# Attention with query weights split on GpSimd, the query bias on ScalarE, and reordered scores and last blocks

## The chip, the cores and the metric

The kernel runs on one core of a Trainium2 chip. The metric is the device time of the whole program in microseconds. A core has TensorE (matmul, PE in the profile), VectorE (DVE), ScalarE (ACT), GpSimd (POOL) and a queue for transfers on SyncE (SP); each works through its own instruction list in order, and they meet through semaphores.

## The reference, cut to what matters

The program is two transformer blocks on 512 tokens of width 1024. The second one ends with a sliding-window attention of 16 query heads over 4 key/value heads, and that attention is what the change touches:

```
q = (h @ w_q + b_q) * 64 ** -0.5               # 16 heads of 64
s = q @ k.T - slope * dist                     # a block of 128 queries against 256 keys
s = where(band and valid, s, -inf)
m = maximum(max(s), sink)
p = exp(s - m)
denom = sum(p) + exp(sink - m)
o = (p @ v) / denom
return o @ w_o + b_o
```

Before it come the keys and values (`kv`), behind it the last feed-forward network. All is in float32.

## The kernel before, in words

**Layout.** Activations are stored with features on the 128 partitions and the 512 tokens along a row, a width of 1024 being eight tiles of 128x512. A float32 matrix product is made of three matmuls of reduced-precision operands: with W = W_hi + W_lo and X = X_hi + X_lo it adds W_hi X_hi, W_hi X_lo and W_lo X_hi. A *unit* is one output tile of 128 features: eight blocks of 128 input features, 24 matmuls of 512 columns.

**Weights.** They stream through four slots. SyncE loads 512 KB into `raw` for slot s (line 1723) once the slot's last low part is made; ScalarE writes W_hi (`split_hi`, line 221, once the slot's last unit is done); the low part W_lo = raw - W_hi is `split_lo` (line 226) on VectorE. `ahead` makes the split two units before it is due. In the first block eleven such low parts are made on GpSimd instead (line 2249).

**Attention.** The 16 heads are eight pairs, pair t being the two heads (e = 0, 1) of query tile t. Per pair:

- TensorE computes the query tile, one unit (`part`, in pieces between other work). VectorE evacuates it from PSUM times the token's norm into the buffer `AW` (`evacuate`, line 1054, semaphore `evac`), and then adds the bias and scales into `QT` (line 1450, semaphore `q_t`).
- `scores_pe` (line 1283) computes scores in two halves n of two query blocks each, both heads, into banks 2 and 3. The second half needs the first to be evacuated (`s_sc`). `scored` (line 1459) evacuates on VectorE and adds the distance term. `maxima` (lines 1468, 1470) follow for e = 0, 1.
- `exps` (lines 1385, 1389) on ScalarE: exponentials and their sums for one head.
- `normalise` (lines 1478 to 1485) on VectorE divides by the sum, four instructions for one head, semaphore `s_n`.
- `transpose_pe` (line 1295) turns the probabilities, `by_keys` (line 1399) on ScalarE copies them, `values_pe` (line 1308) multiplies with the values. ScalarE writes the high part of the output tile (line 1415, `t_hi`), VectorE the low part (line 1491, `t_lo`).

The loop over t runs on each engine by hand-written order: in step t VectorE works on pair t+1's scores and on query tile t+2, TensorE on pair t+1's scores, on unit t+2, and on pair t's transposes and values. The three cuts in `attention_pe` say how many of the eight blocks of unit t+2 stand before the second half's scores, between the transposes, and before the values. Units 8 and 9 are the first two of the output projection (`U_BO`); all but their last two blocks can run inside the loop, and `residual_pe` does the rest.

Of the kernel before, what the change touches and what calls it, by code (L numbers as in the profile page):

```python
# [22 lines left out]
ACT = mybir.ActivationFunctionType  # L23
# [7 lines left out]
KT = D // P  # L31
# [55 lines left out]
def build(nc, io):  # L87
    with ExitStack() as ctx:
# [140 lines left out]
        def split_lo_half(dve, r, s, part):  # L229

            if part == 0:
                dve.wait_ge(S(f"w_hi{s}"), count(f"w_hi{s}", r + 1))
            c = slice(s * 1024 + part * 512, s * 1024 + (part + 1) * 512)
            last = nc.vector.tensor_tensor(w_lo[:, c], raw[:, c], w_hi[:, c].bitcast(F32), ALU.subtract)
            if part:
                last.then_inc(S(f"w_lo{s}"), 1)

        def ahead(eng, split, r, k):
# [819 lines left out]
        def residual_pe(pe, base, pair, wait, n=KT, late=2, begun=False, closing=False):  # L1058
            if begun:
                for s in range(2):  # L1060
                    part_blocks(pe, s, s, pair, n - late, n, n, wait).then_inc(S(f"unit_done{s}"), 1)
            else:
                two_units(pe, rnd(base, 0), pair, wait, late, n)
            for i in range(2):
                for s in range(0 if i else 2, SLOTS - (closing and i)):
                    unit(pe, rnd(base, i), s, pair, n)
# [188 lines left out]
        MX = carve(96)  # L1255
        DD = carve(T)

        def sc3(t, e):
# [54 lines left out]
        def attention_pe(pe):  # L1313
# [32 lines left out]
            scores_pe(pe, 0, 0)  # L1346
            part(1, 2, 5)
            scores_pe(pe, 0, 1)
            part(1, 5, KT)
            part(2, 0, 2)  # L1350
            for t in range(KT):
                cuts = (0, 2, 5, KT) if t else (2, 4, 6, KT)
                if t < KT - 1:
                    scores_pe(pe, t + 1, 0)
                part(t + 2, cuts[0], cuts[1])
                if t < KT - 1:
                    scores_pe(pe, t + 1, 1)
                transpose_pe(pe, t, 0)
                part(t + 2, cuts[1], cuts[2])
                transpose_pe(pe, t, 1)  # L1360
                part(t + 2, cuts[2], cuts[3])
                values_pe(pe, t)

            residual_pe(pe, U_BO, pairA, wait_o, late=2, begun=True)

        def attention_act(act):
# [25 lines left out]
            def by_keys(t, e):  # L1392

                if t > 1:
                    act.wait_ge(S("s_o"), count("s_o", t - 1))
                for n in range(2):
                    act.wait_ge(S("s_tr"), count("s_tr", 4 * t + 2 * e + n + 1))
                    lo = 0 if n else P
                    a.activation(PT[t % 2][e][:, n * T + lo:(n + 1) * T], ps[4 + n][:, lo:T], ACT.Copy)\
                        .then_inc(S("s_pt"), 1)  # L1400
            for k in range(2):
                ahead(act, split_hi, rnd(U_Q, 0), k)
            for e in range(2):
                exps(0, e)
            for t in range(KT):
# [3 lines left out]
                if t < KT - 1:  # L1409
                    exps(t + 1, 0)  # L1410
                by_keys(t, 1)
                if t < KT - 1:
                    exps(t + 1, 1)
# [4 lines left out]
        def attention_dve(dve):  # L1418
            v = nc.vector
            for k in range(2):  # L1420
                ahead(dve, split_lo, rnd(U_KV, 0), k)
# [7 lines left out]
            for e in range(2):  # L1429
                for p in range(2):  # L1430
                    v.memset(SC[p][e][:, 0:P], -FAR).then_inc(S("zeros"), 1)
                v.tensor_copy(DD[:, e * 256:(e + 1) * 256], cst[:, C_DIST:C_DIST + 256]).then_inc(S("zeros"), 1)
            dve.wait_ge(S("zeros"), count("zeros", ZEROS + 6))
            dve.wait_ge(S("kv_R"), count("kv_R", 1))
# [8 lines left out]
            def q_tile(t):  # L1443

                r, k = rnd(U_Q, t // SLOTS), t % SLOTS
                if t:
                    dve.wait_ge(S("q_t"), count("q_t", t))
                evacuate(dve, r, k, AW, 1.0, R[:])
                dve.wait_ge(S(f"evac{k}"), count(f"evac{k}", r + 1))
                v.tensor_scalar(QT[t % 2], AW, par_col("b_q", t), 0.125, ALU.add, ALU.mult).then_inc(S("q_t"), 1)  # L1450

# [41 lines left out]
            q_tile(0)  # L1493
            ahead(dve, split_lo, rnd(U_Q, 0), 0)
            scored(0, 0)
            ahead(dve, split_lo, rnd(U_Q, 0), 1)
            scored(0, 1)
            maxima(0, 0)
            q_tile(1)
            maxima(0, 1)  # L1500
            normalise(0, 0)
            normalise(0, 1)
            for t in range(KT):
                more = t < KT - 1
                if more:
                    scored(t + 1, 0)
                if t < KT - 2:
                    ahead(dve, split_lo, rnd(U_Q, (t + 2) // SLOTS), (t + 2) % SLOTS)
                if t:
                    output_lo(t - 1)  # L1510
                if more:
                    scored(t + 1, 1)
                    maxima(t + 1, 0)
# [179 lines left out]
        def second_block_pool(pool):  # L1693
# [7 lines left out]
            sum_squares(pool, "kv", KT)  # L1701
            token_rsqrt(pool, "kv")
            sum_squares(pool, "n_f1", KT)
            token_rsqrt(pool, "n_f1")
# [693 lines left out]
```

## Time and profile before

| | |
|---|---|
| median of 3 runs | 1967.9 us (1967.87 to 1968.82) |
| profiled execution | 1968.16 us, of which the span of the profile is 1966.1 |
| busy: TensorE | 1894.2 us, 96% |
| busy: VectorE | 1205.2 us, 61% |
| busy: ScalarE | 787.6 us, 40% |
| busy: GpSimd | 280.2 us, 14% |
| mean granted clock of TensorE | 0.988 of full |

The page gives busy time per engine over the whole program, which is an average over stages that differ much. The attention loop takes about 110 us of it, from 1444 to 1553 us. A timeline lists instructions in order of time, with start and duration; in square brackets stands how long the engine had been idle and which engine and line ended that. PEclk in a table of windows is the share of full clock granted to TensorE: 1.00 is 2.4 GHz, 0.50 is 1.2 GHz.

### The profile page before, as it was taken

Reading aid. Unit: us, or ns where it says so; the run is one execution under the profiler, and the core shown is the slowest. Engines: PE = TensorE matmul, PEld = TensorE weight load, DVE = VectorE, ACT = ScalarE, POOL = GpSimd, SP = SyncE. Lnnn points to the kernel's source line nnn. Section 1 sums busy time; section 2 is a strip of 40 time slices with the busy share of each in tenths; the row PEclk is TensorE's granted clock in tenths of the full one; section 3 lists DMA queues with packets and bytes.
Section 4 is the critical chain, followed back from the end, with each engine's and each line's share of the span. In section 5 each row is a group of like instructions: output and inputs, shape, how many; then the busy total and the mean of one; then the engine's idle time right before and its main releaser. Section 6 shows DMA issues by size and latency. Waiting matters only on the chain.

```text
span 1966.1 us, 29676 instructions
## 1 busy us (share of the span) xinstructions
PE 1894.2 (96%) x10634; PEld 1528.4 (78%) x10634; DVE 1205.2 (61%) x1846; ACT 787.6 (40%) x1494; POOL 280.2 (14%) x215
## 2 busy tenths in 40 slices
PE   7999899999999899999989999999999999999997
PEld 5888678888887677777768788888777788888886
DVE  5996544333333777767745756737678657567474
ACT  4233344232233554555533433424536534234242
POOL 2533222011012200000111100101100011001012
PEclk9999999999999899999999999999999999999998
DMA  5232323232323111111112232222311122322322
GB/s 185 94 106 85 109 85 97 96 103 90 106 87 97 44 55 60 60 60 60 50 44 86 97 107 86 96 97 96 125 58 44 63 77 96 110 89 92 103 91 82
DMA packets 46945, 170.47 MB, mean 87 GB/s; under 512 B 5344, under 2 KB 5504, under 8 KB 46720
## 3 DMA queue, kind: packets, MB, share of 16 engines
q1 hardware_dynamic: 45648, 165.12, 25.6%
q10 hardware_dynamic: 1200, 3.95, 0.6%
q8 instruction: 74, 1.21, 0.3%
q14 instruction: 23, 0.19, 0.0%
HBM read 166.94 MB, written 2.11 MB: 86 GB/s over the span
## 4 chain that ended last, share of the span: by engine, by line
PE 75%; DVE 6%; ACT 4%; issue 2%; POOL 1%; DVEq 0%; POOLq 0%; ACTq 0%
PE ps L255 16%; PE ps L256 16%; PE ps L257 16%; PE ps L267 7%; PE ps L269 5%; PE ps L268 5%; DVE scr L1217 1%; PE ps L622 1%; DVE scr L892 1%; ACT scr L1389 1%; ACT Y L1389 1%; PE ps L646 1%; PE ps L666 1%; PE ps L306 1%; DVE scr L1468 1%
## 5 line engine op out<-in xcount | busy, mean ns | idle before, releaser
L226 DVE TENSOR_TENSOR w_lo<-w_raw,w_hi 128x1024 fp32r<-128x1024 f32 x265 | 361.3, 1366 | 184.9 <-ACT w_hi L221 184.8
L221 ACT ACTIVATE w_hi<-w_raw 128x1024 fp32r<-128x1024 f32 x304 | 316.5, 1049 | 244.1 <-PE ps L257 169.2
L255 PE MATMUL ps<-A_hi,w_hi 128*128 128x512 f32 x950 | 369.8, 389 | 2.0 <-issue 1.9
L257 PE MATMUL ps<-A_hi,w_lo 128*128 128x512 f32 x950 | 369.6, 389 | 0.0
L256 PE MATMUL ps<-A_lo,w_hi 128*128 128x512 f32 x950 | 369.6, 389 | 0.0
L255 PE MATMUL ps<-B_hi,w_hi 128*128 128x512 f32 x724 | 282.9, 391 | 3.2 <-issue 2.4
L257 PE MATMUL ps<-B_hi,w_lo 128*128 128x512 f32 x724 | 281.8, 389 | 0.0
L256 PE MATMUL ps<-B_lo,w_hi 128*128 128x512 f32 x724 | 281.8, 389 | 0.0
L255 PEld LDWEIGHTS ps<-A_hi,w_hi 128*128 128x128 f32 x950 | 178.3, 188 | 40.0 <-issue 3.1
L257 PEld LDWEIGHTS ps<-A_hi,w_lo 128*128 128x128 f32 x950 | 178.3, 188 | 37.2
L256 PEld LDWEIGHTS ps<-A_lo,w_hi 128*128 128x128 f32 x950 | 178.3, 188 | 36.8
L267 PE MATMUL ps<-A_hi,w_hi 128*128 128x512 f32 x434 | 188.6, 435 | 18.0 <-DVE w_lo L226 12.7
L269 PE MATMUL ps<-A_hi,w_lo 128*128 128x512 f32 x434 | 171.0, 394 | 0.0
L268 PE MATMUL ps<-A_lo,w_hi 128*128 128x512 f32 x434 | 170.3, 392 | 0.0
L1054 DVE SCALAR_TENSOR_TENSOR scr<-ps,R 128x512 f32<-128x512 f32 x157 | 107.7, 688 | 95.8 <-PE ps L257 86.0
L255 PEld LDWEIGHTS ps<-B_hi,w_hi 128*128 128x128 f32 x724 | 135.9, 188 | 34.4 <-issue 6.3
L257 PEld LDWEIGHTS ps<-B_hi,w_lo 128*128 128x128 f32 x724 | 135.9, 188 | 28.4
L256 PEld LDWEIGHTS ps<-B_lo,w_hi 128*128 128x128 f32 x724 | 135.9, 188 | 27.9 <-issue 0.2
L267 PEld LDWEIGHTS ps<-A_hi,w_hi 128*128 128x128 f32 x434 | 81.9, 189 | 39.7 <-issue 20.1
L1054 DVE SCALAR_TENSOR_TENSOR X<-ps,X 128x512 f32 (+1 forms) x56 | 38.5, 687 | 99.8 <-PE ps L257 88.4
L267 PE MATMUL ps<-B_hi,w_hi 128*128 128x512 f32 x236 | 96.8, 410 | 2.9 <-POOL B_lo L1049 1.7
L269 PEld LDWEIGHTS ps<-A_hi,w_lo 128*128 128x128 f32 x434 | 81.8, 188 | 18.4
(289 smaller groups left out, 2563.7 us busy)
## 6 DMA issues: line engine op xcount, KB each, us to landing
w_raw<-d_ws SPq DMA_DIRECT2D x304, 512.0 KB, 3.5
X<-d_xT SPq DMA_DIRECT2D x4, 512.0 KB, 7.5
X<-d_xT ACTq DMA_DIRECT2D x1, 2048.0 KB, 8.1
d_out<-X SPq DMA_DIRECT2D x4, 512.0 KB, 2.6
scr<-gc_rows ACTq DMA_DIRECT2D x7, 256.0 KB, 3.1
cst<-d_cst SPq DMA_DIRECT2D x1, 800.0 KB, 12.6
par<-d_par SPq DMA_DIRECT2D x1, 344.5 KB, 3.3
scr<-d_pw SPq DMA_DIRECT2D x1, 256.0 KB, 12.4
```

The source lines that it names most:

```text
L221: nc.scalar.activation(w_hi[:, c], raw[:, c], ACT.Copy).then_inc(S(f"w_hi{s}"), 1)
L226: nc.vector.tensor_tensor(w_lo[:, c], raw[:, c], w_hi[:, c].bitcast(F32), ALU.subtract)\
L255: pe.matmul(ps[bank][:], w_hi[:, c], hi, start=k == 0, stop=False)
L256: pe.matmul(ps[bank][:], w_hi[:, c], lo, start=False, stop=False)
L257: last = pe.matmul(ps[bank][:], w_lo[:, c], hi, start=False, stop=k == n - 1)
L267: pe.matmul(ps[bank][:], w_hi[:, c], hi, start=k == 0, stop=False)
L268: pe.matmul(ps[bank][:], w_hi[:, c], lo, start=False, stop=False)
L269: last = pe.matmul(ps[bank][:], w_lo[:, c], hi, start=False, stop=k == total - 1)
L306: pe.matmul(out, w_hi[:, c], tile(pair[0], k), start=k == 0, stop=False)
L622: last = pe.matmul(ps[4 - c // 2][:, (c % 2) * 256:(c % 2 + 1) * 256], KQv[:, c, 0, :], KQ[:, c * 256:(c + 1) * 256], start=True, stop=True)
L1054: return nc.vector.scalar_tensor_tensor(out=out, in0=ps[k % 2 if bank is None else bank][:], scalar=scalar, in1=in1, op0=op0, op1=op1).the ...
L1389: a.activation(sc, sc, ACT.Exp, bias=neg[:, b:b + 1], accum_out=den[:, b:b + 1])\
```

## The change

The low parts of units 2 to 9 of the query and output weights go from VectorE to GpSimd (`split_lo_pool`); from the third on they also wait until pair m - 4 is normalised. VectorE evacuates a query tile as before, but the bias is now added on ScalarE (`query_bias`), with a bias column `QB` that VectorE scales once. In step 0 the second half of pair 1's scores is evacuated before pair 0 is normalised, and TensorE's cuts for steps 0 and 7 and for unit 1 are new. At the end block 6 of both output units stands before block 7 of either.

```diff
@@ -234,6 +234,13 @@
             last = nc.vector.tensor_tensor(w_lo[:, c], raw[:, c], w_hi[:, c].bitcast(F32), ALU.subtract)
             if part:
                 last.then_inc(S(f"w_lo{s}"), 1)
+
+        def split_lo_pool(pool, r, s):
+
+            pool.wait_ge(S(f"w_hi{s}"), count(f"w_hi{s}", r + 1))
+            c = slice(s * 1024, (s + 1) * 1024)
+            nc.gpsimd.tensor_tensor(w_lo[:, c], raw[:, c], w_hi[:, c].bitcast(F32), ALU.subtract)\
+                .then_inc(S(f"w_lo{s}"), 1)
 
         def ahead(eng, split, r, k):
 
@@ -1056,10 +1063,7 @@
 
 
         def residual_pe(pe, base, pair, wait, n=KT, late=2, begun=False, closing=False):
-            if begun:
-                for s in range(2):
-                    part_blocks(pe, s, s, pair, n - late, n, n, wait).then_inc(S(f"unit_done{s}"), 1)
-            else:
+            if not begun:
                 two_units(pe, rnd(base, 0), pair, wait, late, n)
             for i in range(2):
                 for s in range(0 if i else 2, SLOTS - (closing and i)):
@@ -1254,6 +1258,7 @@
         PT = [[carve(2 * T) for _ in range(2)], [Y[:, 2 * (2 + e) * T:2 * (3 + e) * T] for e in range(2)]]
         MX = carve(96)
         DD = carve(T)
+        QB = carve(8)
 
         def sc3(t, e):
             return SC[t % 2][e].rearrange("p (b s) -> p b s", b=NCH)
@@ -1344,24 +1349,31 @@
             part(1, 0, 2)
             pe.wait_ge(S("v_t"), count("v_t", 2))
             scores_pe(pe, 0, 0)
-            part(1, 2, 5)
+            part(1, 2, 4)
             scores_pe(pe, 0, 1)
-            part(1, 5, KT)
+            part(1, 4, KT)
             part(2, 0, 2)
             for t in range(KT):
-                cuts = (0, 2, 5, KT) if t else (2, 4, 6, KT)
+                cuts = (2, 6, 7, KT) if t == 0 else (0, 2, 5, KT) if t < KT - 1 else (0, 1, 3, KT)
                 if t < KT - 1:
                     scores_pe(pe, t + 1, 0)
-                part(t + 2, cuts[0], cuts[1])
+                part(t + 2, cuts[0], cuts[1] - 2 * (t == 0))
                 if t < KT - 1:
                     scores_pe(pe, t + 1, 1)
+                if t == 0:
+                    part(t + 2, cuts[1] - 2, cuts[1])
                 transpose_pe(pe, t, 0)
                 part(t + 2, cuts[1], cuts[2])
                 transpose_pe(pe, t, 1)
                 part(t + 2, cuts[2], cuts[3])
                 values_pe(pe, t)
 
-            residual_pe(pe, U_BO, pairA, wait_o, late=2, begun=True)
+            for k in (KT - 2, KT - 1):
+                for s in range(2):
+                    last = part_blocks(pe, s, s, pairA, k, k + 1, wait=wait_o)
+                    if k == KT - 1:
+                        last.then_inc(S(f"unit_done{s}"), 1)
+            residual_pe(pe, U_BO, pairA, wait_o, begun=True)
 
         def attention_act(act):
             a = nc.scalar
@@ -1398,10 +1410,18 @@
                     lo = 0 if n else P
                     a.activation(PT[t % 2][e][:, n * T + lo:(n + 1) * T], ps[4 + n][:, lo:T], ACT.Copy)\
                         .then_inc(S("s_pt"), 1)
+            def query_bias(t):
+
+                act.wait_ge(S(f"evac{t % SLOTS}"), count(f"evac{t % SLOTS}", rnd(U_Q, t // SLOTS) + 1))
+                if t > 1:
+                    act.wait_ge(S("s_p"), count("s_p", 2 * t - 2))
+                a.activation(QT[t % 2], AW, ACT.Identity, scale=0.125, bias=QB[:, t:t + 1]).then_inc(S("q_t"), 1)
+            query_bias(0)
             for k in range(2):
                 ahead(act, split_hi, rnd(U_Q, 0), k)
-            for e in range(2):
-                exps(0, e)
+            exps(0, 0)
+            query_bias(1)
+            exps(0, 1)
             for t in range(KT):
                 if t < KT - 2:
                     ahead(act, split_hi, rnd(U_Q, (t + 2) // SLOTS), (t + 2) % SLOTS)
@@ -1409,6 +1429,8 @@
                 if t < KT - 1:
                     exps(t + 1, 0)
                 by_keys(t, 1)
+                if t + 2 < KT:
+                    query_bias(t + 2)
                 if t < KT - 1:
                     exps(t + 1, 1)
                 act.wait_ge(S("s_o"), count("s_o", t + 1))
@@ -1417,6 +1439,9 @@
 
         def attention_dve(dve):
             v = nc.vector
+
+            def par_range(name, n):
+                return par[:, _cols[name][0]:_cols[name][0] + n]
             for k in range(2):
                 ahead(dve, split_lo, rnd(U_KV, 0), k)
             for m in range(4):
@@ -1430,7 +1455,8 @@
                 for p in range(2):
                     v.memset(SC[p][e][:, 0:P], -FAR).then_inc(S("zeros"), 1)
                 v.tensor_copy(DD[:, e * 256:(e + 1) * 256], cst[:, C_DIST:C_DIST + 256]).then_inc(S("zeros"), 1)
-            dve.wait_ge(S("zeros"), count("zeros", ZEROS + 6))
+            v.tensor_scalar(QB, par_range("b_q", 8), 0.125, None, ALU.mult).then_inc(S("zeros"), 1)
+            dve.wait_ge(S("zeros"), count("zeros", ZEROS + 7))
             dve.wait_ge(S("kv_R"), count("kv_R", 1))
             for k in range(SLOTS):
                 r = rnd(U_KV, 0)
@@ -1446,8 +1472,6 @@
                 if t:
                     dve.wait_ge(S("q_t"), count("q_t", t))
                 evacuate(dve, r, k, AW, 1.0, R[:])
-                dve.wait_ge(S(f"evac{k}"), count(f"evac{k}", r + 1))
-                v.tensor_scalar(QT[t % 2], AW, par_col("b_q", t), 0.125, ALU.add, ALU.mult).then_inc(S("q_t"), 1)
 
             def scored(t, n):
 
@@ -1491,25 +1515,24 @@
                 v.tensor_tensor(tile(pairA[1], t), ps[6 + t % 2][:], tile(pairA[0], t).bitcast(F32), ALU.subtract)\
                     .then_inc(S("t_lo"), 1)
             q_tile(0)
-            ahead(dve, split_lo, rnd(U_Q, 0), 0)
             scored(0, 0)
-            ahead(dve, split_lo, rnd(U_Q, 0), 1)
             scored(0, 1)
             maxima(0, 0)
             q_tile(1)
             maxima(0, 1)
-            normalise(0, 0)
-            normalise(0, 1)
             for t in range(KT):
                 more = t < KT - 1
                 if more:
                     scored(t + 1, 0)
-                if t < KT - 2:
-                    ahead(dve, split_lo, rnd(U_Q, (t + 2) // SLOTS), (t + 2) % SLOTS)
-                if t:
+                if t == 0:
+                    scored(1, 1)
+                    normalise(0, 0)
+                    normalise(0, 1)
+                else:
                     output_lo(t - 1)
+                    if more:
+                        scored(t + 1, 1)
                 if more:
-                    scored(t + 1, 1)
                     maxima(t + 1, 0)
                     maxima(t + 1, 1)
                     normalise(t + 1, 0)
@@ -1700,6 +1723,10 @@
             ffn_pool(pool, 0, U_FFN0, pairB)
             sum_squares(pool, "kv", KT)
             token_rsqrt(pool, "kv")
+            for m in range(2, 2 + KT):
+                if m > 3:
+                    pool.wait_ge(S("s_n"), count("s_n", 8 * (m - 4) + 8))
+                split_lo_pool(pool, rnd(U_Q, m // SLOTS), m % SLOTS)
             sum_squares(pool, "n_f1", KT)
             token_rsqrt(pool, "n_f1")
             ffn_pool(pool, 1, U_FFN1, pairA)
```

ScalarE, step 1 of the loop, behind pair 1's last transposed half; before (L1399 `by_keys`, L1385 and L1389 `exps` of pair 2's second head, L1415 the output's high part, L221 a weight's high part):

```order
L1399 ACTIVATE Y<-ps 128x384 [waits s_tr]
L1399 ACTIVATE Y<-ps 128x512 [waits s_tr]
L1385 ACTIVATE scr<-scr,small 128x4 [waits s_mx]
L1389 ACTIVATE scr<-scr 128x128
L1389 ACTIVATE scr<-scr 128x256 x3
L1415 ACTIVATE A_hi<-ps 128x512 [waits s_o]
L221 ACTIVATE w_hi<-w_raw 128x1024 [waits unit_done2,raw_in2]
```

After (the same are L1411, L1397, L1401, L1437, L221; L1418 is `query_bias`, waiting for VectorE's `evac3`):

```order
L1411 ACTIVATE Y<-ps 128x384 [waits s_tr]
L1411 ACTIVATE Y<-ps 128x512 [waits s_tr]
L1418 ACTIVATE scr<-scr 128x512 [waits s_p,evac3]
L1397 ACTIVATE scr<-scr,small 128x4 [waits s_mx]
L1401 ACTIVATE scr<-scr 128x128
L1401 ACTIVATE scr<-scr 128x256 x3
L1437 ACTIVATE A_hi<-ps 128x512 [waits s_o]
L221 ACTIVATE w_hi<-w_raw 128x1024 [waits unit_done2,raw_in2]
```

The bias of query tile 3 stands between the transposed half and the exponentials of the second head.

VectorE, from behind pair 2's first normalisation to pair 3's second half of scores; before (L1478 to L1485 `normalise`, L1054 evacuation, L1450 bias, L1459 scores, L226 the weight's low part, L1491 the output's low part):

```order
L1054 SCALAR_TENSOR_TENSOR scr<-ps,R 128x512 [waits unit_done3,q_t]
L1450 TENSOR_SCALAR scr<-scr,par 128x512 [waits evac3]
L1478 TENSOR_TENSOR scr<-scr 128x4 [waits s_e]
L1480 RECIPROCAL scr<-scr 128x4 [waits s_n]
L1484 TENSOR_SCALAR scr<-scr 128x128 [waits s_n]
L1485 TENSOR_TENSOR scr<-scr 128x768
L1459 SCALAR_TENSOR_TENSOR Y<-scr,small,ps 128x384 [waits s_tr,s_p]
L1459 SCALAR_TENSOR_TENSOR Y<-scr,small,ps 128x384
L226 TENSOR_TENSOR w_lo<-w_raw,w_hi 128x1024 [waits w_hi2]
L1491 TENSOR_TENSOR A_lo<-ps,A_hi 128x512 [waits t_hi]
L1459 SCALAR_TENSOR_TENSOR Y<-scr,small,ps 128x512 [waits s_tr,s_p]
L1459 SCALAR_TENSOR_TENSOR Y<-scr,small,ps 128x512
```

After (the same are L1502 to L1509, L1061, L1483, L1515):

```order
L1061 SCALAR_TENSOR_TENSOR scr<-ps,R 128x512 [waits unit_done3,q_t]
L1502 TENSOR_TENSOR scr<-scr 128x4 [waits s_e]
L1504 RECIPROCAL scr<-scr 128x4 [waits s_n]
L1508 TENSOR_SCALAR scr<-scr 128x128 [waits s_n]
L1509 TENSOR_TENSOR scr<-scr 128x768
L1483 SCALAR_TENSOR_TENSOR Y<-scr,small,ps 128x384 [waits s_tr,s_p]
L1483 SCALAR_TENSOR_TENSOR Y<-scr,small,ps 128x384
L1515 TENSOR_TENSOR A_lo<-ps,A_hi 128x512 [waits t_hi]
L1483 SCALAR_TENSOR_TENSOR Y<-scr,small,ps 128x512 [waits s_tr,s_p]
L1483 SCALAR_TENSOR_TENSOR Y<-scr,small,ps 128x512
```

L1450 and L226 are gone from between; the rest keeps its order.

GpSimd, behind the norm of the keys and values, where nothing stood before until the next norm:

```order
L440 TENSOR_TENSOR tok<-tok,mhalf 128x4 [waits norm_ms]
L242 TENSOR_TENSOR w_lo<-w_raw,w_hi 128x1024 [waits w_hi2]
L242 TENSOR_TENSOR w_lo<-w_raw,w_hi 128x1024 [waits w_hi3]
L242 TENSOR_TENSOR w_lo<-w_raw,w_hi 128x1024 [waits w_hi0,s_n]
L242 TENSOR_TENSOR w_lo<-w_raw,w_hi 128x1024 [waits w_hi1,s_n]
L242 TENSOR_TENSOR w_lo<-w_raw,w_hi 128x1024 [waits w_hi2,s_n]
L242 TENSOR_TENSOR w_lo<-w_raw,w_hi 128x1024 [waits w_hi3,s_n]
```

Eight such rows are new; those from the third on also wait for `s_n`.

## Rows read from the trace of the kernel before

**Rows 1.** Timeline of VectorE, one pair: start us, us, instruction [idle before <-releaser].

```profile
1484.04 1.13 DVE L1459 SCALAR_TENSOR_TENSOR Y<-scr,small,ps 128x384 f32<-128x384 f32 x2
1485.10 1.22 DVE L226 TENSOR_TENSOR w_lo<-w_raw,w_hi 128x1024 fp32r<-128x1024 f32 x1
...
1486.83 1.39 DVE L1459 SCALAR_TENSOR_TENSOR Y<-scr,small,ps 128x512 f32<-128x512 f32 x2
...
1491.85 0.16 DVE L1478 TENSOR_TENSOR scr<-scr 128x4 f32<-128x4 f32 x1 [0.84 <-ACT Y L1389]
...
1493.33 0.68 DVE L1054 SCALAR_TENSOR_TENSOR scr<-ps,R 128x512 f32<-128x512 f32 x1
1494.04 0.49 DVE L1450 TENSOR_SCALAR scr<-scr,par 128x512 f32<-128x512 f32 x1
1494.75 0.16 DVE L1478 TENSOR_TENSOR scr<-scr 128x4 f32<-128x4 f32 x1 [0.22 <-ACT Y L1389]
...
1496.23 1.13 DVE L1459 SCALAR_TENSOR_TENSOR scr<-scr,small,ps 128x384 f32<-128x384 f32 x2
```

**Rows 2.** Timeline of VectorE: first evacuations of pairs 2 and 7.

```profile
1471.86 1.13 DVE L1459 SCALAR_TENSOR_TENSOR scr<-scr,small,ps 128x384 f32<-128x384 f32 x2
...
1532.80 1.13 DVE L1459 SCALAR_TENSOR_TENSOR Y<-scr,small,ps 128x384 f32<-128x384 f32 x2
...
1535.16 1.40 DVE L1459 SCALAR_TENSOR_TENSOR Y<-scr,small,ps 128x512 f32<-128x512 f32 x2 [0.64 <-PE ps L1283]
```

**Rows 3.** Timeline of ScalarE, the same pair as rows 1.

```profile
1491.72 0.95 ACT L1399 ACTIVATE scr<-ps 128x384 f32<-128x384 f32 x2
1492.57 0.29 ACT L1385 ACTIVATE scr<-scr,small 128x4 f32<-128x4 f32 x1
```

**Rows 4.** Timeline of ScalarE: two activations of 512 columns.

```profile
1554.14 0.61 ACT L390 ACTIVATE SQ<-X 128x512 f32<-128x512 f32 x1
...
1613.48 0.82 ACT L1164 ACTIVATE scr<-scr,half 128x512 f32<-128x512 f32 x1
```

**Rows 5.** Timelines of ScalarE, of TensorE's weight loads and of VectorE, the start.

```profile
1452.95 0.30 ACT L1385 ACTIVATE scr<-scr,small 128x4 f32<-128x4 f32 x1 [5.87 <-DVE scr L1470]
...
1454.08 0.52 PEld L1283 LDWEIGHTS ps<-scr 64*128 64x128 f32 x8 [0.82 <-DVE scr L1450]
...
1463.77 1.21 DVE L1468 TENSOR_REDUCE scr<-Y 128x4 f32<-128x1024 f32 x1
```

**Rows 6.** Timelines of TensorE and VectorE, the end of the stage.

```profile
1551.49 0.47 PE L267 MATMUL ps<-A_hi,w_hi 128*128 128x512 f32 x1 [0.62 <-DVE A_lo L1491]
...
1552.74 0.74 DVE L1054 SCALAR_TENSOR_TENSOR X<-ps,par,X 128x512 f32<-128x512 f32 x1
...
1553.60 0.19 PEld L255 LDWEIGHTS ps<-A_hi,w_hi 128*128 128x128 f32 x1 [0.22 <-issue]
```

**Rows 7.** Timeline of TensorE, and windows: us, busy of PE, PEld, DVE, ACT, POOL; PEclk, DMA.

```profile
203.09 0.47 PE L1799 MATMUL ps<-B_hi,w_hi 128*128 128x512 f32 x1 [2.82 <-DVE X L2085]
...
1084.68 0.47 PE L255 MATMUL ps<-A_hi,w_hi 128*128 128x512 f32 x1 [1.94 <-issue]
...
1460.32 2.08 PE L1283 MATMUL ps<-scr 64*128 64x256 f32 x8 [3.71 <-DVE Y L1459]
...
1497.42 1.13 PE L1283 MATMUL ps<-scr 64*128 64x256 f32 x8 [0.30 <-DVE scr L1459]
...
202.00:204.00 2.00, 0.91 (x3) 0.80 (x4) 1.86 (x3) 0.00 (x0) 0.00 (x0) 0.87 0.00 0
204.00:206.00 2.00, 2.00 (x6) 1.52 (x6) 0.00 (x0) 0.00 (x0) 0.00 (x0) 0.50 0.41 113
```

**Rows 8.** Timelines of GpSimd and VectorE near 124 us, and the summary of L226.

```profile
124.69 2.40 POOL L2249 TENSOR_TENSOR w_lo<-w_raw,w_hi 128x1024 fp32r<-128x1024 f32 x1 [2.81 <-ACT w_hi L221]
...
122.92 4.69 DVE L2035 SCALAR_TENSOR_TENSOR ps<-Y,par,ps 128x512 f32<-128x512 f32 x7
...
L226 DVE TENSOR_TENSOR w_lo<-w_raw,w_hi x265: 1185/1226/2308, 10.2 to 1942.7; 128x1024 fp32r<-128x1024 f32 x133
```

## Prediction

> **What bounds the kernel now.** I read the page first: TensorE is busy nearly everywhere and the chain that ended last is mostly its, so a change pays only where TensorE waits. The windows over the attention stage (about 1444 to 1553 us) show it waiting there, so I took the timelines of the engines for one pair of head tiles and looked for the engine without holes. That is VectorE [rows 1]. One pair runs from the first score evacuation (L1459, 384 wide) at 1484.04 to the next one's at 1496.23: 12.19 us. VectorE has two holes in it, 0.84 before the first normalisation and 0.22 before the second, both for exponentials. The same step recurs with the same period: 1471.86 to 1532.80 is five pairs, 60.94 us [rows 2]. TensorE waits for VectorE in the same pair (0.30 before the scores at 1497.42 [rows 7]). So the attention stage is one chain: VectorE's evacuations and maxima, ScalarE's exponentials, VectorE's normalisations. The question for each edit is what it does to that chain.
>
> I call pair t the two heads of query tile t. For each pair VectorE normalises half 0, evacuates the query tile two pairs on, and normalises half 1.
>
> **The low parts go to GpSimd.** L226, started at 1485.10, delays what is behind it by 1.13 us (it overlaps its neighbours by 0.1) [rows 1]. It leaves VectorE in each of the five periods. But it was cover: between the first half's evacuation and the second half's, TensorE must compute the second half's scores into the same banks. In the last pair there is no L226, and there the second evacuation waits 0.64 for TensorE: 1535.16 - 1532.80 = 2.36 us from evacuation to evacuation, where a pair with L226 has 1486.83 - 1484.04 = 2.79 [rows 1, 2]. So the gain is 0.43 us per pair, not 1.13. GpSimd needs 2.40 us for such a part [rows 8]; it starts when the pair's normalisation and the high part are done and ends about 0.3 us later than VectorE's did. TensorE reads it two pairs on and the weight slot is refilled for use four pairs on, so this costs nothing on SyncE's queue. If GpSimd fell behind, TensorE's wait for w_lo would show it; it has 12 us for each.
>
> Beside GpSimd's 2.40 us VectorE does the next pair's score evacuation and output part, both with one operand from PSUM. In a stretch where GpSimd splits weights from 124.69, seven such instructions take 4.69 us, 0.67 each, and no longer than elsewhere [rows 8]. I count 0; the other end is L226 itself, which ranges from 1.185 to 2.308 us over the trace. The Trainium skill (GPSIMD Engine Reference, Key points) says GpSimd contends with VectorE instructions that have two SBUF inputs or run in a two-port mode. By it L226 suffers and evacuations don't, as the rows have it; the normalisation would suffer, and the new wait for s_n keeps it out of the way.
>
> **The bias goes to ScalarE.** This is the step that decides. Before, L1450 (0.49 us on VectorE, at 1494.04) ended before ScalarE's second exponentials did: the second normalisation waited 0.22 more for those [rows 1]. Removing it gains nothing on the chain. What comes in its place is on ScalarE, in front of the second exponentials, and waits for VectorE's evacuation (evac), which itself stands behind the first normalisation. ScalarE was ready for the second exponentials at 1492.57, only 0.72 us after the first normalisation began at 1491.85 [rows 1, 3]; the evacuation ends at 1493.33 + 0.68 = 1494.01. From the start of the first normalisation to that of the second:
> before 1494.75 - 1491.85 = 2.90 us [rows 1].
> After: normalisation 1.48 (1491.85 to 1493.33), evacuation 0.68, hand-over 0.03 (ScalarE's first exponentials start that soon behind the maxima), the bias 0.62, exponentials to normalisation 2.18 (1492.57 to 1494.75): 4.99 us. That is 2.09 longer.
> The bias is not in the trace. The nearest rows are Identity of the same width with scale and bias both from a column (0.82) and a square with neither (0.61) [rows 4]; I take 0.72, half-way. The next instruction on ScalarE starts 0.10 before such a one ends (1491.72 + 0.95 against 1492.57 [rows 3]), so 0.62 on the chain, bounds 0.51 and 0.72. The Trainium skill (ScalarE: Activation LUTs, What ACT_TABLE_LOAD costs) gives 280 ns and 0.833 ns an element for a bias from a column, an estimate of 0.71 us for this one; no row here shows it, and the sum doesn't need it. Identity already runs in the same kernel, and the order shows no further table load.
> Net per period 2.09 - 0.43 = 1.66 us, times five: +8.3 us.
>
> **The start.** Two things gain: the second half of pair 0's scores comes after two blocks instead of three (three matmuls; nine take 2.1 us from 1551.49 to 1553.60 [rows 6], so 0.7), and pair 1's scores no longer wait behind pair 0's normalisations. One loses: query_bias(1) stands behind the first exponentials. These begin at 1452.95 - 0.7 = 1452.25 [rows 5] and take 2.1 on ScalarE (2.18 to the normalisation, less the hand-over); the bias then ends 0.72 later at 1455.1, and TensorE, which started these scores at 1454.08 [rows 5], starts at 1455.15. Then 1.13 for the scores, as in the row at 1497.42 [rows 7], 2.36 from evacuation to evacuation and 1.3 for the second one, as in pair 7 [rows 2]: the first normalisation starts at 1459.9, and after two of 1.48 the maxima of pair 1 at 1462.9. Before they started at 1463.77 [rows 5]: 0.9 gained. The 3.71 us wait of TensorE before 1460.32 goes [rows 7]; shorter ones of 1 to 2 us stand in its place. Then the same serial step, 2.09, makes it +1.2 us at the evacuation that started at 1471.86.
>
> **The end.** Pair 7 has no query tile behind it: nothing changes in it. The cuts move blocks behind the last transposes, the same number in all. Running block 6 of both units before block 7 of either fills 0.68 us of TensorE's wait for the last output (0.62 at 1551.49 [rows 6]). But the next unit started at 1553.60, just behind the evacuation of unit 0 (1552.74 + 0.74 = 1553.48), and still needs it: unit 0's last block comes no earlier. I count 0, between 0 and -0.2.
>
> **The sum.** 1.2 + 8.3 + 0 = +9.5 us. The profiled run took 1968.16 us (span 1966.1 and 2.06 around it), the median is 1967.9. So span about 1975.6, profiled run 1977.7, median 1977.4, 0.5% slower. The bounds of the bias (six times 0.1) and of the start and end give 1976.1 to 1978.5 for this case.
>
> **Rivals.**
> *The clock falls.* TensorE's wait before the second half's scores grows from 0.30 (row at 1497.42) by 1.66, and by 0.20 because the query comes that much sooner after the first evacuation (0.43 for the missing L226, less 0.23 by which the bias ends later behind the normalisation, 2.91 against 1494.04 + 0.49 - 1491.85 = 2.68 [rows 1]): 2.16 us. A wait of 2.82 was followed by the lower level (0.50, which is 1.2 GHz) after 204 us, one of 1.94 before 1084.68 was followed by a first matmul at the usual 0.47, and after the one of 3.71 the eight score matmuls took 2.08 instead of 1.13 [rows 7]. So a fall is possible here, and costs 0.95 on the chain at once and some tenths for late transposes. TensorE at half rate then has no spare time in that pair, so at most every second pair: three falls, +3 to +4, 1980.4 to 1981.4. The Trainium skill (TensorE: Matmul & The Clock Gate, What's actually happening) says that an idle TensorE drops to 1.2 GHz and needs sustained work to return; the rows agree, and don't settle 2.16.
> *GpSimd slows VectorE after all.* If evacuations beside it stretch as L226 did at its worst (2.31 for 1.2), the first evacuation pair of 1.04 costs 0.9 more in five periods: +4.6, 1982. Rows 8 speak against it.
> *Not slower: ScalarE isn't held up.* If the evacuation were done by the time ScalarE is through with the transposed half (0.72 after the first normalisation starts, not 2.16), only the gains remain: five times 0.43 and 0.9, -3.1 us, 1964.8. The place is the wait for evac in front of the second exponentials, the point from which it decides is a wait of 1.44 us there. For it speaks that VectorE is the fullest engine and loses work; against it the order, where the bias stands ahead of those exponentials and the evacuation behind the normalisation. TensorE's waits bound what could be gained beyond that: they are under 1 us a pair.
>
> **Chances.** A measurement of this kernel tells no change from one of 0.2%, 3.9 us. The serial step alone 0.66, with falls of the clock 0.16, with GpSimd's contention 0.06, not slower 0.12. The first three are slower by over 0.2% but for a rest: slower 0.87, same 0.10, faster 0.03. The time is that of the first, 1977.4; the range goes down to 1975.0, where the first would end if the serial step were shorter by 0.4 us in each of the six, and up to 1982.5 for the second and third, and leaves the last out.
>
> **What would show it.** In the profile after: the second L1385-line exponentials of pairs 1 to 6 start about 2.8 us after the first normalisation, not 0.7, right behind the bias; ScalarE idles about 1.4 us before the bias, released by VectorE's evacuation; VectorE waits about 2.8 us before each second normalisation (0.22 before); the period is 13.85 us (12.19); the bias takes 0.6 to 0.8; score evacuations beside GpSimd stay at 0.6 to 0.74. Wrong if the period is 12 or less, or if the second normalisations follow the first within 3 us. A period over 15 with a clock below 1.00 in the windows is the second case.

## The result and the profile after

The changed kernel takes 1981.99 us (median of 4 runs, 1980.88 to 1983.11), the kernel before 1968.36 in the same comparison: a ratio of 1.0065 with a 95% interval of 1.0052 to 1.0078. It is slower by 13.6 us. The forecast was 1977.4 us, slower, with a range of 1975.0 to 1982.5. The profiled execution took 1980.88 us, its span is 1979.1, against 1966.1 before.

Timeline of VectorE in the changed kernel, one pair from first score evacuation to first score evacuation (start us, us, instruction, idle before and its releaser); it answers to [rows 1]:

```profile
1515.80 1.13 DVE L1483 SCALAR_TENSOR_TENSOR Y<-scr,small,ps 128x384 f32<-128x384 f32 x2
...
1518.17 1.41 DVE L1483 SCALAR_TENSOR_TENSOR Y<-scr,small,ps 128x512 f32<-128x512 f32 x2 [0.64 <-PE ps L1288]
...
1523.20 0.17 DVE L1502 TENSOR_TENSOR scr<-scr 128x4 f32<-128x4 f32 x1 [0.84 <-ACT Y L1401]
...
1524.68 0.68 DVE L1061 SCALAR_TENSOR_TENSOR scr<-ps,R 128x512 f32<-128x512 f32 x1
1528.20 0.16 DVE L1502 TENSOR_TENSOR scr<-scr 128x4 f32<-128x4 f32 x1 [2.84 <-ACT Y L1401]
...
1529.68 1.13 DVE L1483 SCALAR_TENSOR_TENSOR scr<-scr,small,ps 128x384 f32<-128x384 f32 x2
```

The pair takes 13.88 us instead of 12.19. Evacuation to evacuation is 2.37 (2.79 before), with the 0.64 of waiting for TensorE that [rows 2] showed in the last pair. From the first normalisation to the second (both L1502) it is 5.00 us (2.90 before), and the wait in front of the second went from 0.22 to 2.84 us.

Timeline of ScalarE in the changed kernel, the same pair; it answers to [rows 3]:

```profile
1523.07 0.95 ACT L1411 ACTIVATE scr<-ps 128x384 f32<-128x384 f32 x2
1525.40 0.72 ACT L1418 ACTIVATE scr<-scr 128x512 f32<-128x512 f32 x1 [1.38 <-DVE scr L1061]
1526.03 0.28 ACT L1397 ACTIVATE scr<-scr,small 128x4 f32<-128x4 f32 x1
```

ScalarE is through with the transposed half at 1524.02 and stands still for 1.38 us until VectorE's evacuation is done; the bias takes 0.72, the next instruction follows 0.63 after its start. The exponentials that VectorE waits for begin 2.83 us after the first normalisation, where it had been 0.72.

That is the forecast's mechanism with its numbers. What it did not have is in the stage's first third. VectorE and GpSimd there, then TensorE:

```profile
1461.55 1.22 DVE L1492 TENSOR_REDUCE scr<-Y 128x4 f32<-128x1024 f32 x1
1462.80 1.31 DVE L1494 TENSOR_SCALAR scr<-scr,small 128x4 f32<-128x4 f32 x1
...
1465.26 0.23 DVE L1494 TENSOR_SCALAR scr<-scr,small 128x4 f32<-128x4 f32 x1
```

```profile
1461.71 2.37 POOL L242 TENSOR_TENSOR w_lo<-w_raw,w_hi 128x1024 fp32r<-128x1024 f32 x1 [11.73 <-DVE scr L1509]
```

```profile
1466.72 1.55 PE L1313 MATMUL ps<-scr 128*64 128x128 f32 x22 [3.35 <-ACT scr L1411]
...
1488.21 1.98 PE L1288 MATMUL ps<-scr 64*128 64x256 f32 x8 [2.19 <-DVE Y L1483]
...
1503.11 1.13 PE L1288 MATMUL ps<-scr 64*128 64x256 f32 x8 [2.18 <-DVE scr L1483]
```

L1494, four columns wide, takes 1.31 us instead of 0.23. It ends at 1464.11, as GpSimd's low part of unit 4 does (1464.08). Everything behind it comes 1.08 us later, and TensorE waits 3.35 us in front of pair 0's values. Then its clock falls. Windows of the changed kernel (us, busy of PE, PEld, DVE, ACT, POOL; PEclk, DMA share, GB/s):

```profile
1456.00:1468.00 12.00, 7.24 (x57) 5.42 (x58) 9.61 (x19) 4.64 (x14) 2.37 (x1) 0.99 0.12 45
1468.00:1482.00 14.00, 13.43 (x78) 9.72 (x76) 9.15 (x18) 8.24 (x25) 2.37 (x1) 0.76 0.10 38
1482.00:1496.00 14.00, 11.27 (x70) 8.59 (x67) 8.64 (x19) 8.22 (x25) 2.34 (x1) 0.88 0.11 39
1496.00:1510.00 14.00, 11.82 (x86) 8.82 (x84) 9.38 (x19) 8.13 (x26) 2.35 (x1) 1.00 0.13 39
```

It is granted 0.76 of full in the second and 0.88 in the third, and 1.00 from then on. The second fall comes with a wait of 2.19 us, and costs: the eight matmuls take 1.98 instead of 1.13.

To add it up, the span is cut at the evacuation of query tile 0, at the first score evacuation of pair 2, at that of pair 7 and at the evacuation of output unit 0. All numbers are starts of VectorE's instructions, of the profiled executions:

| us | before | after | difference | forecast |
|---|---|---|---|---|
| up to query tile 0 | 1443.74 | 1442.16 | -1.58 | 0 |
| start, to pair 2 | 28.12 | 30.65 | +2.53 | +1.2 |
| five pairs | 60.94 | 70.75 | +9.81 | +8.3 |
| end, from pair 7 | 19.94 | 19.96 | +0.02 | 0 |
| the rest | 413.36 | 415.58 | +2.22 | 0 |
| span | 1966.1 | 1979.1 | +13.0 | +9.5 |

The five pairs took 14.21, 14.90, 13.88, 13.88 and 13.88 us.

### The profile page after: what moved, and what is told of

Same layout as the page of the kernel before. It is cut to its first block, busy times and chain, and to the rows that moved or that the text cites. A ratio compares the mean times of both kernels' runs of the same rounds, so it can differ in the third digit from the quotient of the medians.

```text
span 1979.1 us, 29689 instructions
## 1 busy us (share of the span) xinstructions
PE 1897.2 (96%) x10634; PEld 1530.6 (77%) x10634; DVE 1195.1 (60%) x1831; ACT 793.1 (40%) x1502; POOL 298.8 (15%) x223
## 4 chain that ended last, share of the span: by engine, by line
PE 75%; DVE 7%; ACT 4%; issue 2%; POOL 1%; DVEq 0%; POOLq 0%; ACTq 0%
PE ps L262 16%; PE ps L263 16%; PE ps L264 16%; PE ps L274 7%; PE ps L276 5%; PE ps L275 5%; DVE scr L1221 1%; PE ps L629 1%; DVE scr L899 1%; ACT scr L1401 1%; PE ps L653 1%; ACT Y L1401 1%; PE ps L1288 1%; PE ps L673 1%; PE ps L313 1%
## 5 line engine op out<-in xcount | busy, mean ns | idle before, releaser
L226 DVE TENSOR_TENSOR w_lo<-w_raw,w_hi 128x1024 fp32r<-128x1024 f32 x257 | 351.6, 1371 | 176.6 <-ACT w_hi L221 176.3
L221 ACT ACTIVATE w_hi<-w_raw 128x1024 fp32r<-128x1024 f32 x304 | 316.5, 1049 | 246.2 <-PE ps L264 169.5
L274 PE MATMUL ps<-A_hi,w_hi 128*128 128x512 f32 x434 | 188.7, 435 | 17.2 <-DVE w_lo L226 12.6
L1061 DVE SCALAR_TENSOR_TENSOR scr<-ps,R 128x512 f32<-128x512 f32 x157 | 107.8, 689 | 102.5 <-PE ps L264 92.5
L1061 DVE SCALAR_TENSOR_TENSOR X<-ps,X 128x512 f32 (+1 forms) x56 | 38.5, 687 | 101.0 <-PE ps L264 88.4
```

Of the source, the lines that this page charges most:

```text
L221: nc.scalar.activation(w_hi[:, c], raw[:, c], ACT.Copy).then_inc(S(f"w_hi{s}"), 1)
L274: pe.matmul(ps[bank][:], w_hi[:, c], hi, start=k == 0, stop=False)
L1061: return nc.vector.scalar_tensor_tensor(out=out, in0=ps[k % 2 if bank is None else bank][:], scalar=scalar, in1=in1, op0=op0, op1=op1).the ...
```

## Experiments

Theory S ("serial step" in the expectations): ScalarE's wait for the evacuation, in front of the second exponentials, is the loss. Theory C: GpSimd's contention with VectorE, and the clock, are. Each kernel was timed beside the kernel before; the medians of before were 1968.56 us in the first four comparisons and 1968.0 in the last four.

**bias_behind.** The changed kernel, the bias behind the exponentials:

```diff
                 by_keys(t, 1)
-                if t + 2 < KT:
-                    query_bias(t + 2)
                 if t < KT - 1:
                     exps(t + 1, 1)
+                if t + 2 < KT:
+                    query_bias(t + 2)
```

> The changed kernel with one edit: from query tile 2 on, the bias stands behind the second exponentials on ScalarE instead of ahead of them. Theory (serial step): the second normalisation again follows the first after 2.9 us instead of 5.0, six times, so 12 us come back less up to 0.3 a pair for the later query: 1968 to 1971 us, period 12 or below. Rival (GpSimd's contention and the clock carry the loss): it stays at 1978 or more.

Measured: 1969.38 us, ratio to before 1.0005 (0.9995 to 1.0014). The pair is 12.18 us. ScalarE's timeline, then TensorE's and VectorE's a little earlier:

```profile
1503.60 0.95 ACT L1411 ACTIVATE Y<-ps 128x384 f32<-128x384 f32 x2
1504.45 0.29 ACT L1397 ACTIVATE scr<-scr,small 128x4 f32<-128x4 f32 x1
...
1506.50 0.71 ACT L1418 ACTIVATE scr<-scr 128x512 f32<-128x512 f32 x1
```

```profile
1495.08 0.93 PE L1288 MATMUL ps<-scr 64*128 64x128 f32 x8 [1.11 <-ACT scr L1418]
```

```profile
1496.05 1.14 DVE L1483 SCALAR_TENSOR_TENSOR scr<-scr,small,ps 128x384 f32<-128x384 f32 x2
...
1498.71 1.41 DVE L1483 SCALAR_TENSOR_TENSOR scr<-scr,small,ps 128x512 f32<-128x512 f32 x2 [0.92 <-PE ps L1288]
```

The exponentials follow the transposed half at once, the bias has no wait. The same work in another place on the same engine gives back 12.6 us of medians. Theory C would have kept the loss. The low part and its early gate are still there: C can't be more than a remainder. But this place is not free either. The query comes later, TensorE waits 1.11 us for it before the next pair's scores (0.50 in the kernel before), and it is 2.66 us from evacuation to evacuation instead of 2.37. So the pair is where it was before the change, and the 0.4 us that the low parts gain are spent.

**bias_dve.** The changed kernel with the bias where it was, on VectorE:

```diff
-            query_bias(0)
...
                 evacuate(dve, r, k, AW, 1.0, R[:])
+                dve.wait_ge(S(f"evac{k}"), count(f"evac{k}", r + 1))
+                v.tensor_scalar(QT[t % 2], AW, par_col("b_q", t), 0.125, ALU.add, ALU.mult).then_inc(S("q_t"), 1)
```

> The changed kernel with the bias back on VectorE, behind the evacuation; low parts on GpSimd and the new orders stay. Theory (serial step): the period falls to about 11.8 us, 1966 to 1970 us in all, depending on what GpSimd's first parts cost at the start. Rival (contention and clock): 1978 or more.

Measured: 1967.47 us, ratio 0.9997 (0.9987 to 1.0007). Four of the five pairs take 11.77 to 11.79 us, 0.40 less than in bias_behind. VectorE:

```profile
1502.06 0.16 DVE L1493 TENSOR_TENSOR scr<-scr 128x4 f32<-128x4 f32 x1 [0.84 <-ACT scr L1401]
...
1504.26 0.49 DVE L1465 TENSOR_SCALAR scr<-scr,par 128x512 f32<-128x512 f32 x1
...
1504.96 0.16 DVE L1493 TENSOR_TENSOR scr<-scr 128x4 f32<-128x4 f32 x1 [0.21 <-ACT scr L1401]
```

From normalisation to normalisation it is 2.90 us with the bias between them, as before: on VectorE it costs nothing on the chain.

**bias_only.** The kernel before with the bias alone moved to ScalarE:

```diff
                 by_keys(t, 1)
+                if t + 2 < KT:
+                    query_bias(t + 2)
                 if t < KT - 1:
                     exps(t + 1, 1)
...
-                v.tensor_scalar(QT[t % 2], AW, par_col("b_q", t), 0.125, ALU.add, ALU.mult).then_inc(S("q_t"), 1)
```

> The kernel before with the bias on ScalarE in the place where the changed kernel has it, nothing else. Theory (serial step): six times 2.1 us over before, period 14.3, some 1980 to 1982 us. Rival (the loss comes from the low parts on GpSimd): 1968, within 0.2% of before.

Measured: 1981.42 us, ratio 1.0069 (1.0053 to 1.0086). This one edit alone makes the kernel 12.9 us slower, with no low part on GpSimd beside the attention. Three of the five pairs take 14.29 us, 2.10 over before, the forecast's 2.09; the other two take 14.85, with the clock down. VectorE's waits:

```profile
1524.21 0.16 DVE L1488 TENSOR_TENSOR scr<-scr 128x4 f32<-128x4 f32 x1 [0.84 <-ACT Y L1390]
1529.22 0.17 DVE L1488 TENSOR_TENSOR scr<-scr 128x4 f32<-128x4 f32 x1 [2.84 <-ACT Y L1390]
```

**split_only.** The kernel before with the low parts on GpSimd:

```diff
-            ahead(dve, split_lo, rnd(U_Q, 0), 0)
             scored(0, 0)
-            ahead(dve, split_lo, rnd(U_Q, 0), 1)
             scored(0, 1)
...
-                if t < KT - 2:
-                    ahead(dve, split_lo, rnd(U_Q, (t + 2) // SLOTS), (t + 2) % SLOTS)
...
+            for m in range(2, 2 + KT):
+                if m > 3:
+                    pool.wait_ge(S("s_n"), count("s_n", 8 * (m - 4) + 8))
+                split_lo_pool(pool, rnd(U_Q, m // SLOTS), m % SLOTS)
```

> The kernel before with the low parts of units 2 to 9 on GpSimd as in the changed kernel, nothing else. Theory (serial step): 0.43 us less a pair, five pairs, and some tenths to 1.3 us for GpSimd's part beside the maxima of pair 1: 1966 to 1968 us. Rival (contention): over 1971, with VectorE instructions beside GpSimd visibly longer in several pairs.

Measured: 1965.32 us, ratio 0.9988 (0.9979 to 0.9998). The pair is 11.78 us, 0.41 less than before for 1.13 us of work taken from VectorE. The median lies 0.7 us below the forecast: the five pairs give 2.0 us, the start takes 28.12 us as before, so the part beside pair 1's maxima that the forecast had charged for did not come, and the rest isn't assigned. Evacuation to evacuation, VectorE:

```profile
1494.11 1.14 DVE L1466 SCALAR_TENSOR_TENSOR scr<-scr,small,ps 128x384 f32<-128x384 f32 x2
...
1496.48 1.41 DVE L1466 SCALAR_TENSOR_TENSOR scr<-scr,small,ps 128x512 f32<-128x512 f32 x2 [0.64 <-PE ps L1290]
```

Here GpSimd's part of unit 4 ran from 1457.98 to 1460.33, beside an evacuation and a wait of VectorE, and L1494's counterpart kept its 0.23 at 1463.70. So the low parts alone don't run into it; the changed kernel's new order at the start, with pair 1's maxima straight behind pair 0's normalisation, brings the two together.

**gate_late.** The changed kernel with GpSimd's part of unit 4 held until pair 1 is normalised:

```diff
-                    pool.wait_ge(S("s_n"), count("s_n", 8 * (m - 4) + 8))
+                    pool.wait_ge(S("s_n"), count("s_n", max(8 * (m - 4) + 8, 16)))
```

> The changed kernel with one edit: GpSimd's low part of unit 4 waits until pair 1 is normalised (s_n 16 instead of 8), so that it no longer runs beside the maxima of pair 1. Theory (a small VectorE instruction, L1494, is held 1.08 us by GpSimd there, TensorE then waits 3.8 us and falls to half clock): the start gets 1 us shorter, the clock stays at 1.00 until later or throughout, 1.1 to 2.5 us less than the changed kernel, 1979 to 1981 us; the period stays 13.9. Rival (the 1.31 us of L1494 is no contention): it stays at 1.31 and the time at 1982.

Measured: 1979.73 us, ratio 1.0059 (1.0044 to 1.0075). The interval overlaps the changed kernel's, so the profile decides. VectorE, then TensorE:

```profile
1462.33 1.21 DVE L1492 TENSOR_REDUCE scr<-Y 128x4 f32<-128x1024 f32 x1
1463.58 0.23 DVE L1494 TENSOR_SCALAR scr<-scr,small 128x4 f32<-128x4 f32 x1
```

```profile
1466.42 1.75 PE L1313 MATMUL ps<-scr 128*64 128x128 f32 x28 [2.27 <-ACT scr L1411]
...
1529.23 1.13 PE L1288 MATMUL ps<-scr 64*128 64x256 f32 x8 [2.19 <-DVE scr L1483]
1544.10 1.83 PE L1288 MATMUL ps<-scr 64*128 64x256 f32 x8 [2.19 <-DVE Y L1483]
```

L1494 is back at 0.23, the start takes 29.56 us instead of 30.65, which is the 1.08, TensorE's wait is 2.27 instead of 3.35, and the clock holds. That the shorter wait is why it holds isn't shown: in best the clock fell behind the same 2.27. Four pairs take 13.88 to 13.89. The clock fell later, near 1530 and 1544, so this run doesn't show what the early falls cost by themselves.

**best.** bias_dve and gate_late together.

> The changed kernel with the bias on VectorE and the later gate for unit 4 together. Theory: 1.1 us or more below the same kernel with the early gate (1967.5): about 1964 to 1966.5, below the kernel before by 0.1 to 0.2%. Rival: the gate gains nothing where TensorE has spare time, 1967.5.

Measured: 1964.06 us (11 runs), ratio to before 0.9981 (0.9972 to 0.9990). It beats both kernels: 17.9 us below the changed one, 3.9 below before. Its start takes 26.24 us (bias_dve 27.25, before 28.12) and its five pairs 59.18 (bias_dve 59.18, before 60.94): 3.6 of the 3.9 us below before. Of the 3.4 us between its median and that of bias_dve, the gate shows only the 1.0 at the start. VectorE at the same place:

```profile
1460.86 0.23 DVE L1485 TENSOR_SCALAR scr<-scr,small 128x4 f32<-128x4 f32 x1
1461.00 1.22 DVE L1483 TENSOR_REDUCE scr<-Y 128x4 f32<-128x1024 f32 x1
```

**evac_first.** The changed kernel, the evacuation ahead of the first normalisation:

```diff
                     maxima(t + 1, 1)
+                    if t + 2 < KT:
+                        q_tile(t + 2)
                     normalise(t + 1, 0)
-                    if t + 2 < KT:
-                        q_tile(t + 2)
```

> The changed kernel with the evacuation of query tile t+2 on VectorE moved ahead of the first normalisation, the bias still ahead of the second exponentials on ScalarE. Theory (what costs is that the evacuation stands behind the normalisation): ScalarE no longer waits 1.4 us, but the unit is finished by TensorE only about 6.9 us after the first score evacuation, so the first normalisation is held instead; the period falls from 13.9 to about 13.0, 4 to 6 us less than the changed kernel, 1976 to 1978 us. Rival (the bias costs by its own time on ScalarE, not by the wait): the period stays at 13.9 or grows.

Measured: 1976.94 us, ratio 1.0040 (1.0025 to 1.0055). Four pairs take 13.27 to 13.29 us, one 14.81 with the clock down. VectorE and ScalarE:

```profile
1522.49 0.69 DVE L1061 SCALAR_TENSOR_TENSOR scr<-ps,R 128x512 f32<-128x512 f32 x1 [1.72 <-PE ps L276]
1523.09 0.15 DVE L1502 TENSOR_TENSOR scr<-scr 128x4 f32<-128x4 f32 x1
...
1526.02 0.16 DVE L1502 TENSOR_TENSOR scr<-scr 128x4 f32<-128x4 f32 x1 [1.37 <-ACT Y L1401]
```

```profile
1523.21 0.72 ACT L1418 ACTIVATE scr<-scr 128x512 f32<-128x512 f32 x1 [0.78 <-DVE scr L1061]
```

The wait for the evacuation shrinks from 1.38 to 0.78, and now TensorE is late: the unit isn't finished, and VectorE waits 1.72 for it with the normalisation queued behind. 0.6 us a pair came back, less than the 0.9 expected; I had the unit finished 6.9 us after the first score evacuation (here at 1514.22); its evacuation could start only after 8.3. The second normalisation follows the first after 2.93 us here, and the pair is still 1.1 us longer than before: the loss has moved in front of the first.

**end_only.** The kernel before with the new cuts of the last step and block 6 of both units ahead of block 7:

```diff
+            for k in (KT - 2, KT - 1):
+                for s in range(2):
+                    last = part_blocks(pe, s, s, pairA, k, k + 1, wait=wait_o)
```

> The kernel before with only the new order at the end: the cuts of the last step and block 6 of both units ahead of block 7. Theory (the next unit waits for unit 0's evacuation either way): no difference, 1968.5 within 1 us, and in the profile the next unit starts as soon after that evacuation as before. Rival (TensorE's wait for the last output is on the path): 0.7 us less.

Measured: 1967.85 us, ratio 0.9997 (0.9988 to 1.0006). VectorE's evacuation of unit 0 and TensorE's next unit:

```profile
1551.33 0.75 DVE L1054 SCALAR_TENSOR_TENSOR X<-ps,par,X 128x512 f32<-128x512 f32 x1
```

```profile
1552.19 0.19 PEld L255 LDWEIGHTS ps<-A_hi,w_hi 128*128 128x128 f32 x1 [0.93 <-issue]
```

The unit starts 0.86 us after the evacuation's start, as in [rows 6] (1552.74 and 1553.60). The matmuls moved ahead only made TensorE's next wait longer: 0.93 where it was 0.22.

## Why the prediction was right, and where it fell short

The step that was to decide is shown, with its size. The sum of the serial step alone, 1976.1 to 1978.5 us, is 3.5 us too low even at its upper end, and that 1981.99 still lies in the range is in part luck: the range went up to 1982.5 for falls of the clock in the loop and for slower evacuations, while much of what came on top was a hold of VectorE at the start and falls of the clock behind the stage, neither of them forecast.

**Low parts on GpSimd.** Right: 0.41 to 0.42 us a pair instead of the forecast's 0.43 (split_only, and 2.37 against 2.79), not the 1.13 that VectorE is relieved of. GpSimd took 2.34 to 2.37 us for each in the loop and was never waited for; the score evacuations beside it kept their length. The contention rival (+4.6 us in the loop) is out.

**The bias.** Right in place and size: 5.00 us between the normalisations (4.99), a bias of 0.72 (0.72), a period of 13.88 (13.85), a wait of 2.84 (2.8). The Trainium skill (ScalarE: Activation LUTs, What ACT_TABLE_LOAD costs) gives an estimate of 0.71 us for the bias; the trace agrees, with 0.71 to 0.72. bias_only shows that this edit makes the loss, bias_behind and bias_dve that it is the place and not the work.

**The start.** Mis-sized: +2.53 us, where the forecast had +1.2. The step that failed is "I count 0" for work beside GpSimd. It looked at the evacuations, which have an operand in PSUM, and had cited from the Trainium skill (GPSIMD Engine Reference, Key points) that GpSimd contends with a two-port mode as well; it did not look at the small tensor_scalar of the maxima, which reads and writes SBUF only (in which mode that runs, no run here shows). It is held for 1.08 us until GpSimd is done, once, because the new gate for unit 4 opens exactly as pair 1's maxima begin. gate_late shows it: 1.09 of the 1.33 us go with it. Most of the rest lies ahead of it: between pair 1's two evacuations it took 2.64 us (1454.63 to 1457.27), where the forecast had 2.36. Wrong as well was that TensorE's wait of 3.71 us would give way to ones of 1 to 2 us: one of 3.35 came, and one of 2.27 where VectorE isn't held.

**The loop.** Five pairs cost +9.81 instead of +8.3. The serial step gives 1.69 a pair, 8.45; the other 1.36 are in the first two pairs (14.21, 14.90), in which the clock was down. So the rival of the falling clock came in beside the serial step, in part, though not as its sign had it (no period is over 15 us): the wait of 2.19 us in front of the second half's scores (forecast 2.16) brought one fall in five, the one in pair 3, and the eight matmuls lost 0.85 there (forecast 0.95); the fall before it followed the longer wait at the start.

**The end.** Right: +0.02 us, and end_only shows why.

**The rest of the span.** -1.58 us before the stage and +2.22 behind it were not forecast, since the instructions there are the same but for one small one (the scaling of the bias column). In the kernels profiled here the stage begins between 1441.74 and 1443.74 us with almost the same code ahead of it; the clock is a part of that: it fell after 203 us before [rows 7] and was 1.00 there in the changed kernel. Behind the stage the clock makes up 2.2 of the 2.22 us, as the last section shows. The profiles are 13.0 us apart and the medians 13.6; the 0.6 between can't be assigned.

## What to carry to other kernels

Before moving an instruction to an engine with spare time, look at what it waits for and at what is queued behind it there: here 0.49 us that cost nothing on the engine that bounds the stage became 2.1 us a pair on a freer one, because the move put a wait for VectorE in front of exponentials for which VectorE itself waits. Behind those exponentials the same instruction still costs 0.4 us a pair (12.18 against 11.78), because TensorE then waits for the query: it was best left where it stood. And taking work off the bounding engine gains only what no other wait takes over, 0.4 of 1.1 us here: read the gap in a pass of the loop in which the work is absent already.

## What the hardware showed beside that

**A four-column instruction can wait for a whole GpSimd instruction.** A tensor_scalar of 128x4 took 1.31 us instead of 0.23 and ended with GpSimd's; the tensor_reduce of 1024 columns before it, also beside GpSimd, took its usual 1.22, and the evacuations from PSUM kept their length too. It is the same in all four kernels with the early gate and the new order (the changed kernel, bias_behind, bias_dve, evac_first): 1.31 us, ending within 0.03 us of GpSimd's instruction. In the other six it takes 0.23.

**A wait of the same length brings the clock down or doesn't.** Four of the kernels have TensorE waits of 2.18 or 2.19 us in front of the second half's scores, 22 in their profiles. Behind 8 of them the granted clock fell (after 1 of 5, gate_late 2 of 6, bias_only 3 of 6, evac_first 2 of 5). The pair then took between 0.6 and 1.5 us longer (bias_only 14.85 against 14.29, evac_first 14.81 against 13.28). Longer waits don't settle it either. Of the four kernels with 3.35 or 3.36 us in front of pair 0's values, the clock fell in the changed kernel and bias_dve and stayed at 1.00 in bias_behind and evac_first.

**The clock fell behind the stage too, in three of the ten kernels.** In the last feed-forward network every kernel has one wait of TensorE of 2.33 to 2.35 us, in front of 240 matmuls. The weight load at its end and a window soon behind it, before and then in the changed kernel:

```profile
1623.44 0.19 PEld L255 LDWEIGHTS ps<-B_hi,w_hi 128*128 128x128 f32 x1 [2.33 <-issue]
1626.00:1628.00 2.00, 2.00 (x11) 1.65 (x10) 1.41 (x2) 1.26 (x2) 0.00 (x0) 1.00 0.09 35
```

```profile
1634.26 0.19 PEld L262 LDWEIGHTS ps<-B_hi,w_hi 128*128 128x128 f32 x1 [2.33 <-issue]
1636.00:1638.00 2.00, 2.00 (x7) 1.51 (x6) 0.95 (x2) 2.00 (x3) 0.00 (x0) 0.50 0.48 184
```

In the changed kernel, bias_only and evac_first the clock was down for about 4 us behind this wait, and the 240 matmuls took 55.9 us; in the other seven it stayed at 1.00, and they took 54.3. That is 1.6 us of the changed kernel's +2.22 behind the stage. The rest is near the very end of the program: eight small matmuls of the last norm take 1.29 us before (from 1953.86, with a clock of 0.69 over 1953 to 1957) and 1.86 after (from 1966.30, with 0.53 over 1966 to 1970). Why the clock fell behind the wait in these three stays open: all three have the longer waits in the attention stage, but so has gate_late, where it held.
